# A two-layer hybrid decoder step: state products, exponentials and sample products in other places

## The reference, cut to what matters

```python
def mixer(h, past_k, past_v, s0, buf, past_len, p):
    z = h @ p['w_in']
    gq, gk, gv, gg, glr, sq, sk, sv, cu = jnp.split(z, offs, axis=-1)
    ...
    o_gla, s_new = gla_chunked(q, k, v, log_a, s0)
    o_gla = rms_norm(o_gla, p['gla_norm'].reshape(GLA_HEADS, GLA_DV)).reshape(B, T, GLA_V)
    ...
    o_sb = stick_breaking(q_sb, k_all, v_all, p['sb_bias'], q_pos, k_pos).reshape(B, T, SB_W).astype(h.dtype)
    ...
    y = jax.nn.silu(layer_norm(y, p['conv_norm_g'], p['conv_norm_b'])).astype(h.dtype)
    mix = jnp.concatenate([o_gla, o_sb, y], axis=-1)
    return mix @ p['w_out'], k_new, v_new, s_new, buf_new
```

## Time and profile before

| | |
|---|---|
| median of 3 runs | 1410.2 us (1409.49, 1410.2, 1413.69) |
| the profiled execution | 1410.71 us, its span 1409.0 us |
| PE busy | 1390.5 us, 99% of the span, 10551 instructions |
| weight loads (PEld) | 1321.0 us, 94% |
| DVE busy | 900.4 us, 64% |
| ACT busy | 736.1 us, 52% |
| POOL busy | 183.2 us, 13% |
| chain that ended last | PE 95%, ACT 2%, DVE 1%, issue 1% |
| granted TensorE clock | 0.999 on average |

### The profile page before, as it was taken

One profiled execution on the slowest core, in us unless ns is written; L12 is line 12 of the kernel. 1 busy time (PEld: TensorE's weight loads), 2 busy tenths in 40 slices (PEclk: granted clock), 3 DMA queues, 4 the chain that ended last, 5 costly groups with the idle time before them and its releaser, 6 DMA issues.

```text
span 1409.0 us, 26946 instructions
## 1 busy us (share of the span) xinstructions
PE 1390.5 (99%) x10551; PEld 1321.0 (94%) x10551; DVE 900.4 (64%) x1508; ACT 736.1 (52%) x1210; POOL 183.2 (13%) x333
## 2 busy tenths in 40 slices
PE   7999999999999999999999999999999999999998
PEld 6999999988878999999999999999888799999998
DVE  5666534669995766663466665446799858756542
ACT  4544444489766554443355444346887665444441
POOL 1020000323263020000000000011433510000000
PEclk9999999999999999999999999999999999999999
DMA  9475455567798595545555554564868995555441
GB/s 245 144 210 151 142 146 155 158 197 228 215 308 258 140 261 150 149 142 152 155 134 150 150 149 138 151 182 138 249 203 242 296 251 155 150 150 148 148 140 51
DMA packets 391554, 249.41 MB, mean 177 GB/s; under 512 B 16513, under 2 KB 379638, under 8 KB 391428
## 3 DMA queue, kind: packets, MB, share of 16 engines
q1 hardware_dynamic: 375602, 204.94, 51.0%
q0 software_dynamic: 15520, 42.62, 9.7%
q10 hardware_dynamic: 306, 0.13, 0.0%
HBM read 242.10 MB, written 5.53 MB: 176 GB/s over the span
## 4 chain that ended last, share of the span: by engine, by line
PE 95%; ACT 2%; DVE 1%; issue 1%; DMA 0%; SPq 0%; DVEq 0%; ACTq 0%
PE bank L596 24%; PE bank L597 24%; PE bank L598 24%; PE bank L860 3%; PE bank L971 2%; PE bank L875 2%; PE bank L636 2%; PE bank L632 2%; PE bank L633 2%; PE bank L1048 1%; PE bank L825 1%; PE bank L1088 1%; PE bank L1090 1%; PE bank L1089 1%; PE bank L952 1%
## 5 line engine op out<-in xcount | busy, mean ns | idle before, releaser
L1599 DVE TENSOR_TENSOR w_l<-raw,w_h 128x1024 fp32r<-128x1024 f32 (+1 forms) x332 | 395.4, 1197 | 291.8 <-ACT w_h L1221 291.5
L596 PE MATMUL bank<-hh,w_h 128*128 128x320 f32 x1632 | 512.5, 314 | 0.0
L598 PE MATMUL bank<-hh,w_l 128*128 128x320 f32 x1632 | 504.3, 309 | 0.0
L597 PE MATMUL bank<-hl,w_h 128*128 128x320 f32 x1632 | 504.1, 309 | 0.0
L1221 ACT ACTIVATE w_h<-raw 128x1024 fp32r<-128x1024 f32 (+1 forms) x332 | 332.4, 1030 | 136.6 <-DMA raw<-in_ffn_w_down 99.9
L596 PEld LDWEIGHTS bank<-hh,w_h 128*128 128x128 f32 x1632 | 306.4, 188 | 10.5 <-issue 8.6
L597 PEld LDWEIGHTS bank<-hl,w_h 128*128 128x128 f32 x1632 | 306.5, 188 | 0.6
L598 PEld LDWEIGHTS bank<-hh,w_l 128*128 128x128 f32 x1632 | 306.3, 188 | 0.0
L596 PE MATMUL bank<-guh,w_h 128*128 128x320 f32 x704 | 217.7, 309 | 0.0
L598 PE MATMUL bank<-guh,w_l 128*128 128x320 f32 x704 | 217.3, 309 | 0.0
L597 PE MATMUL bank<-gul,w_h 128*128 128x320 f32 x704 | 217.3, 309 | 0.0
(11 more groups left out here) (297 smaller groups left out, 1605.9 us busy)
## 6 DMA issues: line engine op xcount, KB each, us to landing
raw<-in_ffn_w_gate SPq DMA_DIRECT2D x88, 512.0 KB, 3.9
raw<-in_ffn_w_up SPq DMA_DIRECT2D x88, 512.0 KB, 3.9
raw<-in_ffn_w_down SPq DMA_DIRECT2D x64, 448.0 KB, 3.7
raw<-in_w_in SPq DMA_DIRECT2D x44, 512.0 KB, 4.0
raw<-in_ffn_w_down SPq DMA_DIRECT2D x32, 512.0 KB, 4.0
kpg<-in_cache_sb_k SPq DMA_DIRECT2D x112, 128.0 KB, 3.2
kpg<-in_cache_sb_k POOLq DMA_DIRECT2D x112, 128.0 KB, 2.7
raw<-in_w_out SPq DMA_DIRECT2D x16, 512.0 KB, 6.3
```

What stands on the lines that cost most here:

```text
L596: pe.matmul(out, w_h[:, slot, k, :], rhs_h[:, k0 + k, :], start=first, stop=False)
L597: pe.matmul(out, w_h[:, slot, k, :], rhs_l[:, k0 + k, :], start=False, stop=False)
L598: last = pe.matmul(out, w_l[:, slot, k, :], rhs_h[:, k0 + k, :], start=False, stop=end)
L1599: V(dve.tensor_tensor(w_l[:, slot, 0:n, :], raw[:, slot, 0:n, :], w_h[:, slot, 0:n, :].bitcast(F32), ALU.subtract), sm["w_lo"])
```

## The change

On each engine's lists:

- `WEIGHTS_AT` runs the exponentials of blocks 0, 1 and 2 (slots 10, 11 and 13 before) in slots 18, 16 and 14, beside those of blocks 5, 4 and 3. One convolution tap of slot 13 moves from before `place_prompt` to behind the log weights. From slot 14 on PE turns values before the level's products.
- `gla_samples` is split from `gla_outputs`. For heads 2 and 3, samples 0 to 3 stay in front of `turn_weights(4)`, and samples 4 to 7, with the `o_prod` signals, come behind the pz products. The means of the two heads move behind the convolution's mean.
- Pair 1 of the state products moves from the mixer to the norm, as the third pair there, in bank 0; `new_states` handles pairs 1, 3, 2 in `settle_in`, ahead of and between the low parts, and sums the squares after them. Waits follow (`st_done`, `r_ready`).

```diff
-TAPS_EARLY = {13: 1, 14: 1, 15: 1, 16: 1, 17: 1, 18: 1, 19: 1}
-TAPS_LATE = {9: 2, 10: 2, 11: 2, 12: 1, 14: 2, 16: 2, 18: 2, 19: 1, 20: 3, 21: 2, 22: 2}
+TAPS_EARLY = {14: 1, 15: 1, 16: 1, 17: 1, 18: 1, 19: 1}
+TAPS_LATE = {9: 2, 10: 2, 11: 2, 12: 1, 13: 1, 14: 2, 16: 2, 18: 2, 19: 1, 20: 3, 21: 2, 22: 2}
...
-WEIGHTS_AT = {10: 0, 11: 1, 13: 2, 14: 3, 16: 4, 18: 5, 20: 6, 22: 7}
+WEIGHTS_AT = {14: (2, 3), 16: (1, 4), 18: (0, 5), 20: (6,)}
...
+                        if k2 % 2 and i == 1 and t == 0:
+                            pe.wait_ge(sm["st_done"], 16 * (k2 // 2) + 8)
...
+                    if 14 <= m < 20:
+                        turn_values(m - 14)
                     if 13 <= m < 21:
                         level_prompt(m - 13)
-                    if 14 <= m < 20:
-                        turn_values(m - 14)
...
-                    for b in range(DB):
+
+                def gla_samples(pair, samples):
+
+                    for b in samples:
...
                 gla_outputs((2, 3))
+                gla_samples((2, 3), range(DB // 2))
                 turn_weights(4)
                 outputs(0)
...
                 last.then_inc(sm["po_prod"], 1)
 
-                gla_means((2, 3))
+                gla_samples((2, 3), range(DB // 2, DB))
                 pe.wait_ge(*at("po_done", 1))
                 pe.wait_ge(*at("conv_y", 1))
...
                 last.then_inc(sm["conv_mean"], 1)
+                gla_means((2, 3))
                 new_values(1)
...
                 pe.wait_ge(*at("conv_d", 2))
-                state_products(1)
...
-                pe.wait_ge(*at("st_done", 8))
+                pe.wait_ge(*at("st_done", 4))
...
                 state_products(3)
+                pe.wait_ge(sm["r_ready"], 3 * M1 + 2)
+                state_products(1)
                 ffn(2 * l + 1, 3 * l + 2, U + U_FFN2)
...
-                sum_squares(M)
-                for q in range(4 if M % 3 == 2 else 5, 8):
-                    lo(u0 + q)
-                    if M % 3 == 2 and q == 5:
-                        new_states(M // 3, (2, 3))
+                if M % 3 == 2:
+                    new_states(M // 3, (1,))
+                    lo(u0 + 4)
+                    new_states(M // 3, (3,))
+                    lo(u0 + 5)
+                    new_states(M // 3, (2,))
+                    sum_squares(M)
+                    lo(u0 + 6)
+                    lo(u0 + 7)
+                else:
+                    sum_squares(M)
+                    for q in range(5, 8):
+                        lo(u0 + q)
...
-                new_states(l, (0, 1))
+                new_states(l, (0,))
...
-S_BANK = (2, 3, 1, 2)
+S_BANK = (2, 0, 1, 2)
+STATE_ORDER = (0, 2, 3, 1)
```

More of the change, by code:

```diff
@@ L1045, in gla_outputs, with mm @@
                 def gla_outputs(pair):
-                    def mm(h, cols, lhs, rhs, first=False, end=False):
-                        return pe.matmul(bank[O_BANK[h % 2]][:, cols], lhs, rhs, start=first, stop=end, skip_group_check=True)
+                    def mm(h, cols, lhs, rhs, first=False):
+                        return pe.matmul(bank[O_BANK[h % 2]][:, cols], lhs, rhs, start=first, stop=False, skip_group_check=True)
                     vh = [slice(h * DV, (h + 1) * DV) for h in range(H)]
@@ L1061, in gla_outputs @@
                             r, p_ = head(h)
-                            last = mm(h, c, st[r, b, p_, :], qt[r, 0, p_, c], end=(b == DB - 1))
+                            last = pe.matmul(bank[O_BANK[h % 2]][:, c], st[r, b, p_, :], qt[r, 0, p_, c], start=False, stop=(b == DB - 1), skip_group_check=True)
                             if b == DB - 1:
@@ L1117, in _ @@
                 gla_outputs((0, 1))
+                gla_samples((0, 1), range(DB))
                 pe.wait_ge(*at("s2_ready", 2))
@@ L1449, in _ @@
                             softplus(h // 2 - 1)
-                    if m in WEIGHTS_AT and m < 22:
-                        weights(WEIGHTS_AT[m])
+                    for it in WEIGHTS_AT.get(m, ()):
+                        weights(it)
                     if m == 9:
@@ L1655, in new_states @@
                 for pair in pairs:
-                    dve.wait_ge(sm["st_prod"], l * per["st_prod"] + pair + 1)
+                    dve.wait_ge(sm["st_prod"], l * per["st_prod"] + STATE_ORDER.index(pair) + 1)
                     for b in (2 * pair, 2 * pair + 1):
```

## The result

The changed kernel takes 1414.67 us, the median of 12 runs (1412.47 to 1418.98), beside 1411.7 for the kernel before on the same chip (12 runs, 1409.1 to 1413.93): a ratio of 1.003, 95% interval 1.0019 to 1.004, so 2.7 to 5.6 us slower. The forecast was 1411.7, 1.5 above the 1410.2 that was known of before, with a range up to 1414.3; the measured median lies 3.0 above the forecast and 0.4 above the range. No change had 0.86 of the chance, slower by over 0.3% had 0.11. In a second set of 11 runs the changed kernel stood at 1414.61, ratio 1.0022 (1.0012 to 1.0032). So it is slower, by about the 0.3% that separates the two words.

The account below looks back on a forecast made before the run. PE, busy for 99% of the span, was taken as the bound. Per layer -0.66 (slots) + 2.38 (second gla heads) - 0.95 (state pair 1) = +0.77, twice +1.5 on 1410.2: 1411.7, range 1408.5 to 1414.3.

Parts of the forecast that it names:

- PE is the bound, and waits at three places: PE busy 99% of the span; it waits in slot 11 (0.50), slot 14 (0.37) and at the mixer's norm (0.65, 0.28).
- The slots: Slots 10 to 22: moved exponentials and tap put PE 0.66 a layer ahead, between 0.50 and 0.87.
- The second gla heads: Split samples: 0.50 idle before the pz products, 1.88 at `po_done`; together 2.38 a layer lost, between 2.2 and 2.8.
- State pair 1: One pair less in the mixer saves 0.95 a layer; at norm and entry cost 0, at most 0.25 and 0.2.
- The sum: A layer: -0.66 + 2.38 - 0.95 + 0 = +0.77, twice +1.5, so 1411.7 against the median of 1410.2.
- Rival (c): The wait of 1.9 at `po_done` drops PE's clock to 1.2 GHz: up to +5 a layer, 1421.7; chance 0.04.
- (a): The split is covered, no wait for `po_done` arises: 1407.0, or 1406.5 with the full lead of 0.87; chance 0.12.
- (b): The slots' lead is lost to DVE's list or late pages, the `po_done` wait stays: 1413.1 to 1413.9; chance 0.18.

Follow-up runs that it names:

- PE kept busy: The changed kernel plus three 128x320 products with unread results between the last sample products and the wait for `po_done`: 1413.36, again 1412.08.
- the pair alone: The kernel before with state pair 1 moved to the mixer's norm and nothing else: 1409.13, ratio 0.9981.
- the tables alone: The kernel before with only the exponentials and convolution tap in their new slots, values still turned after the level's products: 1410.55, ratio 0.9996.
- whole samples in three variants: The changed kernel with samples unsplit: 1407.94; also with the level's products ahead of turning values: 1408.43; with that and ACT's copy ahead of the squares: 1411.28.
- the split alone: The kernel before with only the samples of heads 2 and 3 split and their means behind the convolution's mean: 1415.8, ratio 1.0041.

## Why the prediction was wrong, step by step

**PE is the bound, and waits at three places.** Right. Two of the three waits are gone in the record: the key transposes of slot 11 start 0.15 behind the product before them (311.60 and 311.75), the sample level of slot 14 starts 1.01 behind the scores without a wait.

**The slots, -0.66.** The lead was right: 0.65 at the sample level of slot 15, which starts 1.18 behind the scores where 1.01 is free of waits, so a wait of 0.17 for DVE stands there as foreseen. The step that failed is the one that gave the turning of values a gain of 0.3 and no cost: it costs some 0.04 in each of six slots, and the lead ends at 0.45 to 0.47. So the term was 0.66 in the sum and 0.45 in the records.

**The second gla heads, +2.38.** It came to 2.54 in the clean record (420.28 to 429.16, against 421.45 to 427.79). The wait at `po_done` is 1.83 by the row and 1.90 by the starts (2.89 from the second samples to the mean, 0.99 where nothing waits), forecast 1.88. The idle ahead of the pz products is 0.54, forecast 0.50, but stands elsewhere: PE waits at `outputs(0)` for DVE's copy of `ht`, which in the first record ends at 423.47, 0.33 before the exponentials. The rest is that a second batch of sample products has its own lead-in, 0.1 over its 0.89.

**State pair 1, -0.95.** It saved 0.87: the pair that remains takes 1.02 and not half of 1.89. At the norm every step held. 48 products last until `hh`, the entry starts a little late, no wait for `hl` is left, and `x_mean` is on time by the forecast 0.2: the sum of squares ends at 495.11 + 0.49 = 495.60, and PE takes it at 495.80.

```profile
475.21 2.84 PE L1174 MATMUL bank<-gv,knm 64*64 64x128 f32 x48
477.98 0.41 PE L632 MATMUL bank<-hh,w_h 128*128 128x320 f32 x1
...
479.27 0.85 PE L636 MATMUL bank<-hl,w_h 128*128 128x320 f32 x4
```

```profile
495.11 0.49 DVE L1628 TENSOR_TENSOR sx<-fT 128x320 f32<-128x320 f32 x1
```

**The sum.** Forecast +0.77 a layer; clean records give +1.21 (layer 1 of the second record of the changed kernel) and +0.94 (layer 2 of the second record with PE kept busy), up to +1.56 where a page for `values(7)` comes late by 0.3. For two layers that is 2.2 to 2.8 in place of 1.5. It agrees with the runs: those with PE kept busy and a clock of 0.999 or more average 1412.4, those of before 1409.9.

**Rival (c), the clock, at 0.04.** This is the step that failed in the mechanism: the forecast put the clock's cost at nothing. The clock fell in the wait or up to 1.3 behind it in five of the six layers that three records of the changed kernel hold, and 13 of 24 runs have a mean clock under 0.998. The reason against it ("waits of 0.65 at the norms left it at its full level") argued from waits a third as long, with long input units before and behind them, to a wait of 1.9 amid the smallest products of the program. The price was half right: 3.0 in the first layer, about 1.6 in the second (2.54 against 0.94), not +5 each time, because the clock comes back before the stretch ends. Both agree with half of the time at half clock: 6.8 less the 0.6 in which PE still waited, and 3.4. The rule of the Trainium skill (TensorE: Matmul & The Clock Gate, "Why this matters for your kernels") asks for no long idle gaps between bursts of products, or the clock goes to half. The two kernels that differ only in the gap bear out its direction. The gaps that it warns of are longer than the 1.83 here, so taken by its letter it would have let this change pass, and the forecast was wrong to call the risk one by that rule; the measurement decides.

**What the base already did.** I took the spread of before (1409.49 to 1413.69) for noise. It goes with the clock: 44 of its 112 runs in four sets have a mean under 0.998 and average 1413.3, 55 have 0.999 or more and average 1409.9. The one profile shown was of the undisturbed kind, so "the granted clock is full until PE has nothing more to do" was true of the record and not of the kernel. It also moves the base: the 12 runs of before beside the result have a median of 1411.7, 1.5 above the 1410.2 of three runs from which the forecast was made, and that is half of the 3.0 by which the forecast missed. And some of what the wait costs, before pays already: the mean of all runs is 1411.4 for before, 1.5 above its undisturbed runs, and 1415.1 for the changed kernel, 2.7 above 1412.4. So the 3.7 between the means are 2.5 of counted work and waits, and 1.2 of clock. With only the terms of the sum mis-sized, 1410.2 + 2.5 = 1412.7 would have stayed in the range.

**Rivals (a) and (b).** (a) named the remedy: with the copy ahead of the squares the time is 1408.4, between its 1407.0 and no change (its 1406.5 for the full lead should read 1406.6: 1410.2 less twice 1.82). (b) did not happen; 0.45 of the 0.66 of the slots' lead was kept.

## What to carry to other kernels

Where a change puts work between two steps of one engine, look at what the other engines have queued between the same two: here one copy behind two squares made a wait of 1.8 out of a piece that should have been free, and moving one line on ACT gave back about 6 us (1414.67 to 1408.38, on two chips). A wait of the matrix engine amid small products costs its length and can cost more by the clock: here 2.0 on average behind two waits of 1.83, and up to 3.0 behind one. So price it at both. And when the runs of a kernel spread by more than a few tenths of a per cent, list their mean clocks before the spread is taken for noise: a single record shows one of the two kinds.

## What the runs showed of the hardware

- The granted clock goes to half not only behind a wait. In nine places, in records of eight kernels (before, the changed one, the pair alone, the tables alone, PE kept busy by three products, and whole samples in three variants), it falls for 3.4 us while PE is busy without a break, each time 0.2 to 0.8 behind the end of a batch of 32 instructions of 64x8. Input units of long products never showed it. Which runs it meets was not settled: it differs between executions of the same kernel.
- A wait of 1.83 in the same place was followed by a fall in layer 2 alone (second record), in both layers (two records) or in none (the split alone). In three of the five falls the clock went down 0.6 to 0.7 before the wait ended and stayed down for 6.8 us; in the other two it went down 1.2 to 1.3 after the end (in the first record the mean starts at 1122.7 and the clock is low from 1124.0) and stayed down for 3.4.
- With the clock at half behind the wait DMA moved nothing for 6 us (share 0.00 at 430 to 436); in the layer with the wait and no fall it was some 4 us (0.00 and 0.02 at 428 to 432). The page for `values(7)` came up to 0.3 late in other kernels (in layer 1 its 32 products take 2.14 with the copy first and 2.24 in the second record with PE kept busy, instead of 1.93), but not in the records of the changed kernel (1.93 in layer 1), so the two are not shown to belong together.
